# Forgetting attention's scores in two 128-row passes per head instead of four 64-row passes

## The reference

```python
q = (xn @ w_q).reshape(B, T, 16, 64)          # k, v, c come from kvf = rms_norm(h, kv_norm) @ w_kvf
for i in range(T // BLK):                     # BLK = 128
    s = einsum('bqhd,bkhd->bhqk', q[:, q0:q1], k[:, :q1]) * 64 ** -0.5
    s = s + (c_t[:, :, q0:q1, None] - c_t[:, :, None, :q1])   # c: cumulative log forget gates
    s = where(causal, s, NEG)
    p = softmax(s, axis=-1)
    outs.append(einsum('bhqk,bkhd->bqhd', p, v[:, :q1]))
h = h + rms_norm(o @ w_o, g[1])
```

## Time and profile before

| | |
|---|---|
| median of 3 runs | 2225.47 us (2223.09 to 2225.75) |
| the profiled execution | 2217.3 us, span of the core 2215.5 us |
| granted TensorE clock, mean | 0.975 |
| PE busy | 2083.5 us, 94% of the span |
| DVE busy | 1443.1 us, 65% |
| ACT busy | 598.6 us, 27% |
| POOL busy | 1165.1 us, 53% |
| chain that ended last | PE 83%, DVE 9%, ACT 4% |

### The profile page before, as it was taken

The page is one execution under the profiler, slowest core; times in us unless marked ns, Lnnn a source line. Parts: engine busy times, 40 slices in busy tenths (PEclk is TensorE's granted clock), DMA queues, the critical chain, the costliest instruction groups (busy, mean ns, idle before and its releaser), DMA issues.

```text
span 2215.5 us, 33463 instructions
## 1 busy us (share of the span) xinstructions
PE 2083.5 (94%) x13910; PEld 1724.1 (78%) x13910; DVE 1443.1 (65%) x1852; ACT 598.6 (27%) x1239; POOL 1165.1 (53%) x664
## 2 busy tenths in 40 slices
PE   6989999999999989999999989989889888999998
PEld 5877788888877767787887668878788677888886
DVE  7767778377765546779578697878666755611622
ACT  2243220121235453220121132356424222200200
POOL 6723767666655444766665334544300555656654
PEclk9999999999999999999999999999999998999999
DMA  5311335334422112334435331212100112333321
GB/s 185 112 47 57 105 105 178 107 95 166 143 67 67 56 31 76 102 114 140 142 98 185 133 106 49 67 39 96 39 3 4 59 57 67 96 95 100 100 86 67
DMA packets 55767, 201.94 MB, mean 91 GB/s; under 512 B 6560, under 2 KB 6816, under 8 KB 54720
## 3 DMA queue, kind: packets, MB, share of 16 engines
q1 hardware_dynamic: 52272, 187.23, 26.1%
q0 software_dynamic: 1840, 9.60, 1.2%
q10 hardware_dynamic: 1504, 2.95, 0.5%
HBM read 194.78 MB, written 4.19 MB: 90 GB/s over the span
## 4 chain that ended last, share of the span: by engine, by line
PE 83%; DVE 9%; ACT 4%; issue 2%; POOL 1%; DMA 0%; ACTq 0%; SPq 0%; DVEq 0%; POOLq 0%
PE bank L536 69%; PE bank L2857 1%; PE bank L2853 1%; PE bank L2842 1%; POOL parts_r L517 1%; PE bank L3121 1%; PE bank L1436 1%; PE bank L1930 1%; PE bank L1742 1%; PE bank L1942 1%; PE bank L1423 1%; PE bank L1413 1%; ACT xn L2933 1%; DVE big L2107 0%; POOL parts_r L511 0%
## 5 line engine op out<-in xcount | busy, mean ns | idle before, releaser
L536 PE MATMUL bank<-xn_r,parts_r 128*128 128x512 f32 (+1 forms) x2928 | 912.4, 390 | 31.4 <-DVE mix_r L764 14.3
L536 PE MATMUL bank<-big_r,parts_r 128*128 128x512 f32 x3208 | 924.4, 391 | 2.2 <-POOL parts_r L517 2.2
L517 POOL TENSOR_TENSOR parts_r<-ring,parts_r 128x1024 fp32r<-128x1024 f32 x293 | 740.9, 2529 | 24.4
L511 POOL TENSOR_SCALAR parts_r<-ring 128x1024 fp32r<-128x1024 f32 x293 | 346.0, 1181 | 719.6 <-PE bank L536 708.3
L536 PEld LDWEIGHTS bank<-big_r,parts_r 128*128 128x128 f32 x3208 | 601.7, 188 | 133.4 <-issue 4.7
L536 PEld LDWEIGHTS bank<-xn_r,parts_r 128*128 128x128 f32 x2928 | 551.5, 190 | 155.9 <-issue 36.9
L891 ACT ACTIVATE big<-bank,small 128x512 f32<-128x512 f32 x88 | 68.3, 779 | 410.9 <-DVE big L935 252.3
L920 DVE TENSOR_TENSOR bank<-bank,nb 128x512 f32<-128x512 f32 x88 | 61.3, 699 | 142.5 <-PE bank L536 142.4
L3388 DVE SCALAR_TENSOR_TENSOR h<-bank,vecs,h 128x512 f32<-128x512 f32 x24 | 17.9, 751 | 173.6 <-PE bank L536 173.6
L3462 DVE TENSOR_TENSOR big<-big 128x512 f32<-128x512 f32 x32 | 82.7, 2585 | 70.8 <-ACT big_r L3443 70.8
L547 DVE TENSOR_TENSOR big_r<-big,big_r 128x512 fp32r<-128x512 f32 x76 | 105.8, 1394 | 0.4
(11 more groups left out here) (463 smaller groups left out, 2779.9 us busy)
## 6 DMA issues: line engine op xcount, KB each, us to landing
ring<-weights SPq DMA_DIRECT2D x295, 512.0 KB, 3.6
cst<-mod_w SPq DMA_DIRECT2D x48, 512.0 KB, 3.8
h<-x SPq DMA_DIRECT2D x8, 256.0 KB, 6.5
h_store<-h POOLq DMA_DIRECT2D x8, 256.0 KB, 2.3
big<-consts POOLq DMA_DIRECT2D x2, 1024.0 KB, 8.8
h<-h_store POOLq DMA_DIRECT2D x1, 2048.0 KB, 9.1
out<-mix SPq DMA_DIRECT2D x8, 256.0 KB, 2.2
cst<-consts SPq DMA_DIRECT2D x1, 1300.0 KB, 10.9
```

Of the source, the lines that this page charges most:

```text
L511: pool.tensor_scalar(rounded(unit_parts(u)[0]), ring[:, u % RING], 1.0, 0.0, ALU.mult, ALU.add)\
L517: pool.tensor_tensor(rounded(lo), ring[:, u % RING], value(hi), ALU.subtract).then_inc(part_ready, 1)
L536: mm = pe.matmul(ps, rounded(w[a]), rounded(x[b]), start=(start and n == 0), stop=(stop and n == 2))
```

## The change

Each head's scores are now two passes over all 128 rows. Of four 512-column tiles per parity of the pair's number, `K_PARTS` holds for each head the pair of tiles [K hi over K lo] and [K hi over the gate rows], `Q_BOTH` holds [Q hi over Q hi], and `Q_REST` [Q lo over selector]: the first pass gives hi by hi plus hi by lo, the second lo by hi plus the gates. That takes twice the tiles, and those of the odd pairs lie in the residual `h`, which is written to DRAM (`h_store`) by SP before and read back after the last scores.

The work around it: ACT writes the selector's rows for each pair (two copies of 64x512), K hi twice over for each head (two copies of 64x1024), Q hi (two of 64x512) and Q hi again on the other half's rows (two of 64x512); before it wrote K hi and Q hi as one 128x512 copy each, and rounded all selectors once. K lo moves from POOL to DVE (`k_lo`, two subtractions of 64x512, in the first task of the next pair), Q lo stays on POOL as two subtractions of 64x512 that follow each other by a semaphore (`q_lo`). `kq_take` writes two raw buffers in place of four tiles.

```diff
+        def kq_tiles(pair, first, n):
+            if pair % 2:
+                return h[:, first:first + n]
+            return kq_spare[first // 4][:, first % 4:first % 4 + n]
+        K_PARTS, Q_BOTH, Q_REST = (0, 2), (4, 5), (6, 7)
+        b_raw = (nb[:, 0], nb[:, 5])
...
         def kq_hi(act, i):
-            slot = kq_slot(i % 2, i // 2)
+            pair, c = divmod(i, 2)
+            if c == 0:
+                if i >= 4:
+                    act.wait_ge(*after("b_scores", 2 * PAIR * (pair - 1)))
+                for g in range(2):
+                    r = half_rows[1 - g]
+                    act.activation(rounded(kq_tiles(pair, Q_REST[g], 1)[r, 0]).rearrange("p (m n) -> p m n", n=P),
+                                   b_sel[r, 2 * pair + g].unsqueeze(1).broadcast_to((HD, TB, P)), ACT.Copy)
             act.wait_ge(sem("b_kqt"), i + 1)
-            act.activation(rounded(b_kq_hi[:, slot]), b_kq_lo[:, slot], ACT.Copy).then_inc(sem("b_kqh"), 1)
+            for g in range(2):
+                r = half_rows[g]
+                if c == 0:
+                    ins = act.activation(rounded(kq_tiles(pair, K_PARTS[g], 2)[r]),
+                                         b_raw[0][r].unsqueeze(1).broadcast_to((HD, 2, T)), ACT.Copy)
+                else:
+                    ins = act.activation(rounded(kq_tiles(pair, Q_BOTH[g], 1)[r, 0]), b_raw[1][r], ACT.Copy)
+            ins.then_inc(sem("b_kqh"), 1)
+            if c:
+                for g in range(2):
+                    ins = act.activation(rounded(kq_tiles(pair, Q_BOTH[g], 1)[half_rows[1 - g], 0]), b_raw[1][half_rows[g]], ACT.Copy)
+                ins.then_inc(sem("b_kqd"), 1)
+
+        def k_lo(dve, pair):
+            dve.wait_ge(sem("b_kqh"), 2 * pair + 1)
+            for g in range(2):
+                own = kq_tiles(pair, K_PARTS[g], 1)[:, 0]
+                ins = dve.tensor_tensor(rounded(own[half_rows[1 - g]]), b_raw[0][half_rows[g]], value(own[half_rows[g]]), ALU.subtract)
+            ins.then_inc(sem("b_klo"), 1)
+
+        def q_lo(pool, pair):
+            pool.wait_ge(part_ready, UNITS["b_kq"] + PARTS + (2 * pair if pair else -1) + 1)
+            pool.wait_ge(sem("b_kqh"), 2 * pair + 2)
+            for g in range(2):
+                r = half_rows[g]
+                pool.tensor_tensor(rounded(kq_tiles(pair, Q_REST[g], 1)[r, 0]), b_raw[1][r],
+                                   value(kq_tiles(pair, Q_BOTH[g], 1)[r, 0]), ALU.subtract).then_inc(sem("b_qlo"), 1)
+                pool.wait_ge(sem("b_qlo"), 2 * pair + g + 1)
...
@@ pair_scores
             if t % PAIR == 0:
-                pe.wait_ge(sem("b_kql"), 2 * pair + 2)
-            ps = [grab(pe, g, *after("b_masked", 2 * t + g + 1)) for g in range(2)]
+                pe.wait_ge(sem("b_klo"), pair + 1)
+                pe.wait_ge(sem("b_qlo"), 2 * pair + 2)
+                pe.wait_ge(sem("b_kqd"), pair + 1)
             own = slice(tb * P, (tb + 1) * P)
-            for g, r in enumerate(half_rows):
-                pe.matmul(ps[g][:, 0:w], rounded(b_sel[r, 2 * pair + g]), rounded(b_c[r, 0:w]), start=True, stop=False)
-            for n, (of_q, of_k) in enumerate(((b_kq_hi, b_kq_hi), (b_kq_hi, b_kq_lo), (b_kq_lo, b_kq_hi))):
-                for g, r in enumerate(half_rows):
-                    mm = pe.matmul(ps[g][:, 0:w], rounded(of_q[r, q_, own]), rounded(of_k[r, k_, 0:w]), start=False, stop=(n == 2))
-                    if n == 2:
-                        mm.then_inc(sem("b_scores"), 1)
+            for g in range(2):
+                ps = grab(pe, g, *after("b_masked", 2 * t + g + 1))
+                k_, k_c = (kq_tiles(pair, K_PARTS[g], 2)[:, n, 0:w] for n in range(2))
+                pe.matmul(ps[:, 0:w], rounded(kq_tiles(pair, Q_BOTH[g], 1)[:, 0, own]), rounded(k_), start=True, stop=False)
+                pe.matmul(ps[:, 0:w], rounded(kq_tiles(pair, Q_REST[g], 1)[:, 0, own]), rounded(k_c), start=False, stop=True)\
+                  .then_inc(sem("b_scores"), 1)
...
@@ b_dve
                 if kq_done(t) is not None:
                     kq_take(dve, kq_done(t))
+                elif kq_done(t - 1) is not None and kq_done(t - 1) % 2 == 0:
+                    k_lo(dve, kq_done(t - 1) // 2)
...
@@ mixb_act, before b_act
-            act.activation(rounded(cst[:, T:T + B_HEADS * P]), cst[:, T:T + B_HEADS * P], ACT.Copy)\
-               .then_inc(sem("b_sel"), 1)
+            for i in range(2):
+                kq_hi(act, i)
+            act.wait_ge(*after("b_c", 1))
+            act.wait_ge(sem("h_kept"), 16)
+            act.wait_ge(*after("b_xnl", KD))
+            for g in range(2):
+                r = half_rows[1 - g]
+                act.activation(rounded(kq_tiles(1, K_PARTS[g], 2)[r, 1]), value(kq_tiles(0, K_PARTS[g], 2)[r, 1]), ACT.Copy)
+            for i in range(2, 2 + KQ_AHEAD // 2):
...
@@ mixb_dve
+            dve.wait_ge(sem("h_kept"), 32)
             out_dve(dve, "b", "g11", ("g12", ffn_x, "ffn1_xn"), bank0=2)
...
@@ sync
+                if u == UNITS["b_v1"] + RING:
+                    sp.wait_ge(*after("ffn0_h", KD))
+                    sp.dma_start(h_store[:, :], h.rearrange("p k t -> p (k t)")).then_inc(sem("h_kept"), 16)
+                if u == UNITS["b_o"] + KD - 1:
+                    sp.wait_ge(*after("b_scores", 2 * b_n))
+                    sp.dma_start(h.rearrange("p k t -> p (k t)"), h_store[:, :]).then_inc(sem("h_kept"), 16)
...
@@ gpsimd
-            kq_lo(pool, 0)
             for i in range(2 * KD):
-                if i < 2:
-                    kq_lo(pool, i + 1)
-                elif i > 2:
-                    kq_lo(pool, i)
+                if i == 0 or (i % 2 and i > 1):
+                    q_lo(pool, i // 2)
```

More of the change, by code:

```diff
@@ L1327, in mixa_dve @@
             out_dve(dve, "a", "g01", ("g02", ffn_x, "ffn0_xn"))
-        b_kq_hi = part(0, 4, T)
-        b_kq_lo = xn_all[:, KD * T:KD * TA].rearrange("p (k t) -> p k t", k=4)
+        kq_spare = (part(0, 4, T), xn_all[:, KD * T:KD * TA].rearrange("p (k t) -> p k t", k=4))
+        def kq_tiles(pair, first, n):
[4 more added lines that the diff above has]
+        b_raw = (nb[:, 0], nb[:, 5])
         b_v, b_o = part(4 * T, TB, D), part(4 * T + TB * D, KD, T)
@@ L1343, in build @@
         b_PT = [[big[:, b_work + 4 * T:b_work + 5 * T], nb[:, 1]], [nb[:, 2], nb[:, 3]]]
-        def kq_slot(c, pair):
-            return 2 * c + pair % 2
         def kq_part(pe, pair, ks):
@@ L1392, in kq_lo @@
[L1392 to L1396, removed]
+            if i >= 2 and i % 2 == 0:
+                dve.wait_ge(sem("b_klo"), i // 2)
+            if i >= 2 and i % 2:
+                dve.wait_ge(sem("b_qlo"), 2 * (i // 2))
+                dve.wait_ge(sem("b_kqd"), i // 2)
@@ L1600, in mixb_pe @@
             pe.wait_ge(*after("b_c", 1))
-            pe.wait_ge(sem("b_sel"), 1)
             b_pe(pe)
@@ L1624, in mixb_act @@
             act.wait_ge(cst_in, 32)
-            act.activation(rounded(cst[:, T:T + B_HEADS * P]), cst[:, T:T + B_HEADS * P], ACT.Copy)\
-               .then_inc(sem("b_sel"), 1)
             act.activation(stat[:, 15:16], gain("eps"), ACT.Exp)
-            for i in range(2 + KQ_AHEAD // 2):
+            for i in range(2):
[7 more added lines that the diff above has]
+            for i in range(2, 2 + KQ_AHEAD // 2):
                 kq_hi(act, i)
@@ L1651, in mixb_dve @@
             dve.wait_ge(cst_in, 32)
-            c_rows = lambda a, b: rounded(b_c[a:b])
-            link(dve, dve.tensor_scalar(c_rows(0, P), cst[:, 0:T], 0.0, None, ALU.mult))
-            dve.tensor_copy(c_rows(HD, HD + B_HEADS), z)
+            c_of = [kq_tiles(0, K_PARTS[g], 2)[:, 1] for g in range(2)]
+            c_rows = lambda at, n: rounded(c_of[0 if at >= HD else 1][at:at + n])
+            first_of = lambda at: value(c_of[0 if at >= HD else 1][at:at + B_HEADS])
+            dve.tensor_scalar(c_rows(HD, HD), cst[HD:P, 0:T], 0.0, None, ALU.mult)
+            link(dve, dve.tensor_scalar(c_rows(0, HD), cst[0:HD, 0:T], 0.0, None, ALU.mult))
+            dve.tensor_copy(c_rows(HD, B_HEADS), z)
             link(dve, dve.tensor_copy(c_rows(0, B_HEADS), z))
-            dve.tensor_tensor(c_rows(HD + 32, HD + 32 + B_HEADS), z, value(b_c[0:B_HEADS]), ALU.subtract)
-            dve.tensor_tensor(c_rows(32, 32 + B_HEADS), z, value(b_c[0:B_HEADS]), ALU.subtract).then_inc(sem("b_c"), 1)
+            dve.tensor_tensor(c_rows(HD + 32, B_HEADS), z, first_of(0), ALU.subtract)
+            dve.tensor_tensor(c_rows(32, B_HEADS), z, first_of(0), ALU.subtract).then_inc(sem("b_c"), 1)
             for i in range(2 + KQ_AHEAD // 2):
                 kq_take(dve, i)
+                if i == 1:
+                    k_lo(dve, 0)
             b_dve(dve)
+            dve.wait_ge(sem("h_kept"), 32)
             out_dve(dve, "b", "g11", ("g12", ffn_x, "ffn1_xn"), bank0=2)
```

7 lines of the change are left out of this document (1 added, 6 removed).

## The result

The changed kernel is slower by 0.95%: ratio of the times 1.0095, 95% interval 1.0076 to 1.0114; medians 2246.74 us and, beside it on the same chip, 2225.28. I had forecast 2231.7 with a range up to 2238, so the sign was right and the size was not: 21 us lost where I had 6.

What follows compares the result with a forecast made beforehand. With PE full but its 6.4 us gain hidden, the alternation of DVE and ACT was to bound the attention pairs: +2.1 us over six periods, +2.5 start, +1.6 end, +6.2 on 2225.47, so 2231.7 us, range 2220 to 2238.

Steps and rivals of the forecast that it cites:

- PE's gain: Attention scores on PE: one switch of tiling goes, 0.2 us a task, a pair from 20.16 to 19.35 us.
- Alternation: DVE and ACT taking turns in every attention task: needs 20.2 to 21.2 us a pair, taken as 20.5 against 20.16.
- queries' copies on ACT: Four copies where one was, at 0.54 us each: 1.6 us more a pair, 1.5 of it on the chain.
- keys' copies on ACT: Two selector and two double-width copies where one was, ahead of the exponentials: 1.0 us more a pair (0 to 1.0).
- keys' subtractions on DVE: Two subtractions for the keys' small part in the first task: 1.3 us a pair (0.6 to 1.4).
- port waits, net: DVE and POOL in a pair: one port wait less, -0.6 us, but other waits for POOL 0.6 to 1.6 more.
- Six periods by 0.35: First to last pair: 6 full periods, each +0.35 us against 20.16, together +2.1 us (-1.8 to +6.0).
- Start: First pair: double-width copies +1.4, subtractions +1.3, port 0 to 1.0, scores by head saving 0.5; taken as +2.5 us.
- End: Last pair: POOL's part of the first stashed output stands behind three more ACT copies, +1.6 us (0.5 to 1.6).
- Transfers and selector rounding at nothing: The residual's save and reload are covered, and dropping the rounding of all selectors (1.91 us) gives nothing back.
- the copies are covered: Rival: ACT and DVE stay under 19.35 us a pair, PE shows its 6.4 us, 2219.5 us; chance 0.17.
- the subtractions meet POOL: Rival: the port holds the keys' subtractions half a split each time, 8.4 us more, 2240 us; chance 0.06.

Runs made afterwards that it cites:

- x_klo: e_place with only the keys' subtractions put back on DVE ahead of the 512-column task's mask: 1.0038 of the kernel before, pair 20.30 us.
- after_fill2: The changed kernel with spare PE matmuls at two places of the last pair: 1.0078 of the kernel before, stage 180.4 us.
- e_dma: The kernel before with only the residual's save to DRAM, its reload and DVE's wait for it added: 1.0004 of the kernel before, pair 20.14 us.
- e_place: The changed kernel, all work kept, with ACT's added copies and the keys' subtractions moved to where their engine waits: 1.0003 of the kernel before, pair 19.40 us.
- e_best: e_place with the stage's start and end reordered too (POOL's split first, last queries on three engines): 1.0011 of the kernel before.

## Why the prediction was wrong

**PE's gain** (0.2 us a task, 20.16 to 19.35): right; 19.40 where nothing hides it.

**Alternation**, the step that failed: its sum gave 20.5 us a pair (19.85 to 21.15) and the pair took 22.22. Its form, one sum over the pair against PE's own pace, holds where DVE never waits for PE, as in the changed kernel; what failed there are the sizes. Its terms against the earlier trace rows:

| term, us a pair | forecast | measured |
|---|---|---|
| queries' copies on ACT | 1.5 | (731.17 - 728.09) - (719.11 - 718.09) = 2.06 |
| keys' copies on ACT | 1.0 | 741.81 - 740.22 = 1.6 |
| keys' subtractions on DVE | 1.3 | 1.42 |
| port waits, net | about +0.3 | (0.94 - 0.35) + (1.30 - 0.17) + (0.85 - 0.29) + (0.54 - 0.17) = 2.65, less 1.63 before = +1.0 |
| the rest | 16.4 | what is left: 22.22 - 2.06 - 1.6 - 1.42 - 1.0 = 16.1 |

(0.35, 0.17, 0.29 and 0.42 are the lengths of these operations away from POOL's work, the first in x_klo, the others in rows shown here; before, (0.83 - 0.35) + (0.66 - 0.17) + (1.08 - 0.42) = 1.63.) Every added term was short, the port's by 0.7, the queries' and the keys' copies by 0.6 each. ACT's copies of 64 rows follow each other by 0.64 us and not 0.54, the double-width ones take 1.05: I had taken the distance of one pair of rows for all. And I took 20.5 out of 19.85 to 21.15, "since a tie decides it"; three operations of DVE in a row met POOL's work, where I had let one slip ahead of it.

**Six periods by 0.35**: a misreading of before. The last of them was 17.98 us and not 20.16, since PE has 36 passes of projection there in place of 48; the new order took 22.21 all the same, so +4.2 in place of +0.35. The view that would have shown it is PE's first scores for all eight pairs, of which I had read two.

**Start** +2.5 against +4.3: the port was put at 0 to 1.0. In the changed kernel's first task the two-column operation takes 1.82 us and the scaling of 128 columns 2.36, at a clock of 1.00, where before they took 0.17 and 0.34: 3.7 us more, or 2.0 with the wait of the earlier trace rows, which is gone there (0.17 for 1.82). The terms on ACT and DVE were not tested one by one. **End** +1.6: the first output product came 3.7 us behind the last pair's scores before (804.37 - 800.70) and as much after (824.86 - 821.14), so the term was nothing by itself. The +2.2 of this execution goes with its clock: with the clock at 1.00 (after_fill2) the last part was 26.5.

**Transfers and selector rounding at nothing**: right for the transfers (e_dma); the rounding was not tried. **Rivals**: "the copies are covered" needed another order, which e_place gave in the steady part, though start and end took the gain back (1.0003); "the subtractions meet POOL" did not happen in the steady part (1.39 us for both, POOL idle), as argued.

## What to carry to other kernels

When two engines hand work to and fro, add up their order over a whole period, waits for a shared port included, and compare it with the bound engine's period: a piece placed directly on that order counts once the sum is above, however idle the engines look, and by its lateness it can push later pieces into the shared port. In e_place the same pieces cost the steady pair nothing in the gaps where one engine waits for the other. A difference of two periods is the cost of a piece only if the same order bounds both; the waits for PE tell. Read every period of the stage, the first and the last above all: here the last one was 2.2 us shorter than the others before the change and no shorter after it.

## What the runs showed of the hardware

POOL and DVE also hold each other up where both subtract in SBUF. In e_best DVE's two subtractions of 64x512, 1.39 us in the changed kernel, took 2.37 beside POOL's, and POOL's two took 3.28 where they need 2.65:

```profile
682.63 2.37 DVE L1446 TENSOR_TENSOR h_r<-nb,h_r 64x512 fp32r<-64x512 f32 x2
```

```profile
682.85 3.28 POOL L1461 TENSOR_TENSOR h_r<-nb,h_r 64x512 fp32r<-64x512 f32 x2 [11.53 <-ACT h_r L1437]
```

The Trainium skill, SBUF — State Buffer, section SBUF: two separate sides, says that a DVE operation with two SBUF inputs is locked out while a GpSimd operation that reads SBUF holds the port, and the other way round; these rows agree, with 1.0 us for DVE and 0.6 for POOL.

A copy on 64 rows is no shorter on ACT than one on 128: two of 512 columns took 1.27 us together, and the earlier trace rows show 0.63 for one on 128 rows.
